# Two transformer blocks on one core: the list of a pair of experts turned in another PSUM bank, a fourth buffer for rounded expert weights, and first feed-forward products ahead of the second turning of the modulation rows

## The reference

```python
def swiglu(h, w13, w2):
    a, b = jnp.split(h @ w13, 2, axis=-1)
    return (jax.nn.silu(a) * b) @ w2

def half_ffn(x, g, shift, scale, gate, w13, w2):
    return x + 0.5 * gate * swiglu(modulate(x, g, shift, scale), w13, w2)

def grouped_moe(h, router_w, router_b, w_gate, w_up, w_down):
    ...                      # sigmoid router; two experts per token out of one group of four
    for e in range(N_EXPERTS):
        he = jax.nn.silu(t @ w_gate[e]) * (t @ w_up[e])
        y = y + combine[:, e:e + 1] * (he @ w_down[e]).astype(jnp.float32)
```

## Time and profile before

| | |
|---|---|
| median of 3 runs | 2240.47 us (2235.95 to 2245.8) |
| profiled execution: own time | 2240.65 us |
| its span, first to last instruction | 2238.9 us |
| busy share PE, DVE, ACT | 96%, 69%, 48% |
| mean granted TensorE clock | 0.989 |

### The profile page before, as it was taken

The page is one execution under the profiler, slowest core; times in us unless marked ns, Lnnn a source line. Parts: engine busy times, 40 slices in busy tenths (PEclk is TensorE's granted clock), DMA queues, the critical chain, the costliest instruction groups (busy, mean ns, idle before and its releaser), DMA issues.

```text
span 2238.9 us, 31572 instructions
## 1 busy us (share of the span) xinstructions
PE 2141.5 (96%) x13334; PEld 1898.6 (85%) x13334; DVE 1555.5 (69%) x1626; ACT 1081.2 (48%) x1197; POOL 6.7 (0%) x16
## 2 busy tenths in 40 slices
PE   9999999998999999989999999899999999999998
PEld 7888888768999999989999889777777888777777
DVE  4896676336867777747776555787787545787877
ACT  4222231336434534445444645566666555666665
POOL 0000000000000000000000000000000000000000
PEclk9999999999999999999999999999999999999999
DMA  8676867523878688645887333688887333777886
GB/s 320 203 243 240 291 214 255 215 74 120 303 292 301 228 295 308 223 151 207 298 300 268 133 113 132 241 304 304 306 318 293 113 114 113 281 296 297 322 306 226
DMA packets 143105, 535.25 MB, mean 239 GB/s; under 512 B 11744, under 2 KB 47912, under 8 KB 115184
## 3 DMA queue, kind: packets, MB, share of 16 engines
q1 hardware_dynamic: 141280, 524.33, 64.6%
q0 software_dynamic: 944, 5.72, 0.6%
q10 hardware_dynamic: 736, 3.12, 0.4%
HBM read 532.06 MB, written 1.06 MB: 238 GB/s over the span
## 4 chain that ended last, share of the span: by engine, by line
PE 74%; DVE 13%; ACT 8%; DMA 3%; issue 2%; SPq 0%; DVEq 0%; ACTq 0%
PE PS L988 16%; PE PS L914 11%; PE PS L1565 9%; DVE moe_low L2916 7%; PE PS L1060 7%; PE PS L1010 7%; PE PS L949 5%; PE PS L1600 5%; PE PS L1115 4%; ACT W_HIGH L2163 2%; DMA moe_ring<-moe_w 2%; ACT h_parts L2163 2%; DVE ring_low L2416 1%; PE PS L807 1%; PE PS L883 1%
## 5 line engine op out<-in xcount | busy, mean ns | idle before, releaser
L988 PE MATMUL PS<-h_parts,FFN_HIGH 128*128 128x256 f32 x2112 | 383.1, 284 | 2.9 <-DVE h_parts L2397 2.9
L2916 DVE TENSOR_TENSOR moe_low<-moe_ring,W_HIGH 128x2048 fp32r<-128x2048 f32 x128 | 293.1, 2291 | 81.6 <-ACT W_HIGH L2163 81.3
L988 PEld LDWEIGHTS PS<-h_parts,FFN_HIGH 128*128 128x128 f32 x2112 | 329.0, 192 | 3.7 <-issue 3.4
L988 PE MATMUL PS<-h_parts,ring_low 128*128 128x256 f32 x1056 | 298.7, 283 | 0.0
L2163 ACT ACTIVATE W_HIGH<-moe_ring 128x2048 fp32r<-128x2048 f32 x128 | 244.7, 1914 | 66.8 <-PE PS L1565 33.7
L2424 DVE TENSOR_TENSOR ring_low<-ring,FFN_HIGH 128x2048 fp32r<-128x2048 f32 x99 | 226.8, 2290 | 37.7 <-ACT FFN_HIGH L1827 37.6
L2455 DVE SCALAR_TENSOR_TENSOR roots<-CB,cond_rows,roots 128x1024 f32<-128x1024 f32 x186 | 238.4, 1282 | 9.0
L1827 ACT ACTIVATE FFN_HIGH<-ring 128x2048 fp32r<-128x2048 f32 x99 | 189.1, 1910 | 97.2 <-DMA ring<-down_w 87.6
L988 PEld LDWEIGHTS PS<-h_parts,ring_low 128*128 128x128 f32 x1056 | 202.6, 192 | 0.0
L1565 PE MATMUL PS<-moe_low,HXH 128*128 128x512 f32 x504 | 200.1, 397 | 0.0
L2916 DVE TENSOR_TENSOR moe_low<-moe_ring,h_parts 128x2048 fp32r<-128x2048 f32 x64 | 146.4, 2288 | 34.6 <-ACT h_parts L2163 34.4
(11 more groups left out here) (388 smaller groups left out, 4670.9 us busy)
## 6 DMA issues: line engine op xcount, KB each, us to landing
moe_ring<-moe_w SPq DMA_DIRECT2D x192, 1024.0 KB, 5.2
CB<-mod_rows SPq DMA_DIRECT2D x192, 512.0 KB, 5.8
ring<-up_w SPq DMA_DIRECT2D x88, 1024.0 KB, 4.9
ring<-lin_w SPq DMA_DIRECT2D x55, 1024.0 KB, 4.8
ring<-down_w SPq DMA_DIRECT2D x43, 1024.0 KB, 5.8
CB<-mod_dual SPq DMA_DIRECT2D x96, 128.0 KB, 2.6
ring<-mod_w SPq DMA_DIRECT2D x8, 1024.0 KB, 8.4
CB<-mod_rows SPq DMA_DIRECT2D x32, 128.0 KB, 2.7
```

The source lines that it names most:

```text
L988: return mm(PS[:, i % 2, h * S:(h + 1) * S], a[:, k, h * P:(h + 1) * P], b[:, k, :], start=start, stop=(k == KT - 1 and j == 2), skip_grou ...
L2916: tt(by_tile(moe_low[:, moe_slot(l, p), :]), by_tile(moe_ring[:, moe_slot(l, p), :]), w_high_tiles(p), ALU.subtract).then_inc(w_low, 1)
```

## The change

There are three edits.

1. `turn_list` of the next pair writes PSUM bank 2 instead of 3. TensorE waits ahead of it for `mo_g` of the odd expert's first half (bank 2 emptied by `gated(e, 0)`), and the wait for `mo_placed` moves from `gate_up(e, 2)` of the odd expert to `gate_up(e, 0)` of the next even one, the next writer of bank 2.
2. A third flat buffer of rounded parts, so four with `H_HIGH`. All `split` calls of ScalarE and VectorE stand where they stood, but handle the unit one further ahead (`+ 4` for `+ 3`), with one more split ahead of the loop over the experts. ScalarE's wait for the buffer is for the end of unit `p - 4`. The ring of loads keeps its five slots.
3. The two groups of spare products ahead of `up0` go. `up0` starts on the first half of the modulations, and `turn_rows(1)` stands behind the first six products (`k == 0`).

```diff
-        W_FLAT = [rounded(f"W_HIGH{i}", G_at + (at + i * UW) * 4, [P, UW]) for i in range(2)]
-        at += 2 * UW
+        W_FLAT = [rounded(f"W_HIGH{i}", G_at + (at + i * UW) * 4, [P, UW]) for i in range(3)]
+        at += 3 * UW
...
-            return (W_FLAT[i % 3][:, :].rearrange("p (k c) -> p k c", k=KT) if i % 3 < 2 else H_HIGH)
+            return (W_FLAT[i % 4][:, :].rearrange("p (k c) -> p k c", k=KT) if i % 4 < 3 else H_HIGH)
...
-                keep_busy(0, 4)
-                pe.wait_ge(mods_ready, 1)
-                turn_rows(1)
-                keep_busy(0, 8)
...
-                pe.wait_ge(mods_ready, 2)
+                pe.wait_ge(mods_ready, 1)
...
+                            if k == 0:
+                                turn_rows(1)
+                        last.then_inc(unit_done, 1)
+                        pe.wait_ge(mods_ready, 2)
...
-                    if i == 2 and e % 2 and q + 1 < PAIRS:
-                        pe.wait_ge(mo_placed, q0 + q + 2)
+                    if i == 0 and e and e % 2 == 0:
+                        pe.wait_ge(mo_placed, q0 + q + 1)
...
-                        turn_list(q + 1, 3)
+                        pe.wait_ge(mo_g, 2 * (e0 + e) + 1)
+                        turn_list(q + 1, 2)
...
-                    act.wait_ge(unit_done, u0 + p - 2 if p >= 3 else u0)
+                    act.wait_ge(unit_done, u0 + p - 3 if p >= 4 else u0)
...
-                    split(MOE_AT[e, 0] + 3)
+                    split(MOE_AT[e, 0] + 4)
                     gate(e, 0)
-                    split(MOE_AT[e, 1] + 3)
+                    split(MOE_AT[e, 1] + 4)
                     if e:
-                        split(MOE_AT[e - 1, 4] + 3)
+                        split(MOE_AT[e - 1, 4] + 4)
                         if e % 2 and q + 1 < PAIRS:
-                            listed(q + 1, 3)
+                            listed(q + 1, 2)
                         if e % 2 == 0:
                             outputs(q - 1)
-                        split(MOE_AT[e - 1, 5] + 3)
-                    split(MOE_AT[e, 2] + 3)
+                        split(MOE_AT[e - 1, 5] + 4)
+                    split(MOE_AT[e, 2] + 4)
                     gate(e, 1)
-                    split(MOE_AT[e, 3] + 3)
+                    split(MOE_AT[e, 3] + 4)
```

More of the change, by code:

```diff
@@ L926, in up0 @@
                                     last = part(h, k, j)
-                    last.then_inc(unit_done, 1)
+                        last.then_inc(unit_done, 1)
                     sums(0, i)
@@ L2206, in moe @@
                 listed(0, 5)
+                split(3)
                 for e in range(NE):
@@ L2976, in moe @@
                     gated(e, 0)
-                    split(MOE_AT[e, 1] + 3)
+                    split(MOE_AT[e, 1] + 4)
                     if e:
-                        split(MOE_AT[e - 1, 4] + 3)
+                        split(MOE_AT[e - 1, 4] + 4)
                         if e % 2 and q + 1 < PAIRS:
-                            placed(q + 1, 3)
+                            placed(q + 1, 2)
                         if e % 2 == 0:
                             outputs(q - 1)
-                        split(MOE_AT[e - 1, 5] + 3)
+                        split(MOE_AT[e - 1, 5] + 4)
                     if e % 4 == 0 and group + 1 < GROUPS:
                         lists(group + 1)
-                    split(MOE_AT[e, 2] + 3)
+                    split(MOE_AT[e, 2] + 4)
                     gated(e, 1)
-                    split(MOE_AT[e, 3] + 3)
+                    split(MOE_AT[e, 3] + 4)
                     if e % 2 == 0 and group + 1 < GROUPS:
```

## The result

| | before | changed |
|---|---|---|
| median of the runs, us | 2238.39 (4 runs, 2235.95 to 2245.8) | 2313.51 (4 runs, 2311.29 to 2320.72) |
| profiled execution: own time / span | 2240.65 / 2238.9 | 2320.72 / 2318.8 |
| mean granted TensorE clock | 0.989 | 0.971 |

The changed kernel is slower: ratio 1.0335, 95% interval 1.03 to 1.0371, 75 us by the medians. The forecast was 2274 us with 2300 as the high end of its range. The direction was forecast, the size was not.

The account below looks back on a forecast made before the run. TensorE, busy 96% of 2238.9 us, was taken to bound the kernel; 2240.65 - 2.5 (start) + 4 (odd halves) + 26 (even halves) + 6 (clock) = 2274 us. Its own range was 2252 to 2305, the stated range 2238 to 2300.

Parts of the forecast that it names:

- Edit 1, 23.2 us if nothing else is late: Mixtures, list in the other bank: 14 TensorE waits of 1.66 us for `placed` go, saving 23.2 us.
- Edit 3, -2.5: Program start: `up0` begins earlier, saving 2.5 us; bounds 0, if a later feed-forward chain takes it, and 2.7.
- Edit 2, the mechanism: Mixtures: splits wait for loads, some 30 us or more per mixture, delaying `gated` some 2.2 us and list compare 2.6.
- The clock, "+6, four of the 16": TensorE in the mixtures: four of 16 new waits bring half clock, 1.5 us each: +6 us, bounds 0 and 24.
- slower, by the clock: Rival: nearly every new wait brings 3.4 us at half clock, 2268 + 24 = 2292 us; inside the forecast's 0.70.
- The landing, 5.2 us: Expert loads in the mixtures: median time from issue to landing, 5.2 us, at least 4.7; used in both halves' terms.
- The odd halves, "14 x (L - 4.9)": Odd halves of the mixtures, L the landing: 14 x 0.3 = +4 us instead of -23.
- The even halves, 16 x 1.6 = 26: Even halves of the mixtures: late splits delay list compare and gathered rows, mean 1.6 us over 16 halves, +26 us.
- The range: Whole kernel: 2252 us (loads at 4.7, no clock lost) to 2305 (loads at 5.7, half of the clock cost).
- the case without change: Rival: VectorE catches up after late splits, only half of the 26 arrives; 2244 us, 2235 to 2250, chance 0.15.
- The faster rival, "the loads are in time": Mixtures: loads land before ScalarE reaches the split, edit 2 costs nothing, edits 1 and 3 win; 2215 us, chance 0.15.
- break-even of 4.3 us: Load landing in the mixtures at which 14 x -0.6 + 16 x 0.7 - 2.5 is about nothing, deciding the faster case.

Follow-up runs that it names:

- the spare products: Changed kernel plus eight unused products ahead of odd experts' turned products and ahead of the gathering that waits for the list: 2312.03 us, ratio 1.0306.

## Why the prediction was right in direction and wrong in size

- **Edit 1, 23.2 us if nothing else is late: right.** 23.0 alone by the medians, 19.7 by the lengths.
- **Edit 3, -2.5: right at its place, wrong in the end.** The first unit ends 2.5 us earlier; the median does not move (2244.89 against 2244.34). The bound of 0 "if a later chain takes it" is what the profile shows, at 1229 us rather than in the first feed-forward.
- **Edit 2, the mechanism: right.** The splits wait for loads: 72 and 77 us per mixture for "some 30 or more", in about 8 pieces per pair for "12 or so". The loss comes through `gated` ahead of the turned products of odd experts (2.98 for 2.2 in the half worked out), and through the list compare (2.68 for 2.6). Splits three ahead with the same buffers remove nearly all of it.
- **The clock, "+6, four of the 16": the step that failed.** 22 stretches of half clock in the mixtures for 2 before, 82 us more, worth some 35 us by the table above. I had only one wait in the trace of before to go by, 2.01 with a fall, and the 1.66 without one. The new waits are 1.8 to 4.6 us; of those of 2.2 and more, 20 of 24 have a stretch in or behind them. The rival "slower, by the clock" counted 24 us for it and ended at 2292, still short, since it priced one stretch per odd half and four list waits, and the even halves' other waits not at all.
- **The landing, 5.2 us: too short for the loads that matter, the second mis-sized term.** The 28 loads on the chain took 5.65 on average, which adds 13 us. The median of 5.2 is over all loads, also those that nothing waits for.
- **The odd halves, "14 x (L - 4.9)": the form right.** Before, odd halves took 18.4 to 18.5 us (and one 20.0); after, up to 20.1 in the first mixture and 22.1 in the second (sums of seven, the last of each mixture left out: 136.0 and 142.9 against 129.2 and 130.8). Of these 18.9 us of growth over 14 halves the form at L = 5.2 makes 3, where the forecast said 4; the longer landings (5.56 on average here) make 5 and the half clock 11.
- **The even halves, 16 x 1.6 = 26: right at its own landing.** The seven even halves went from 156.7 and 155.5 us to 179.9 and 187.1 in sum: 55 us over 14, 2.1 to 7.4 each. Without half clock and with landings of 5.2 the growth would be 23 (the rest of these halves taken from the kernel with loads of half the bytes), where 14 x 1.6 is 22; the longer landings (5.75) make 8 and the half clock 24.
- **The sum.** 3 and 23 for the landing as forecast, 13 for longer landings, 35 for the clock: the 74 us by which the mixtures grew. The clock's part is not won back by mending it alone, since the landings then grow, as the spare products show. Both go when the landing is no longer waited for: 98 us between distances three and four.
- **The range.** Its high end, 2305, does not follow from its terms: loads at 5.7 and half of the clock's 24 give 2240.65 - 2.5 + 45 + 12 = 2295. In the case without change, the -3 and the +9 are added with no row behind them; half of the 26 would be 13.
- **The faster rival, "the loads are in time", with its break-even of 4.3 us:** with landings of 3.7 the kernel is faster than before by 12 us (0.9931), not by the 25 of the rival. Of the 86 us by which that run's lengths are shorter than the changed kernel's, 50 are its 28 shorter landings (28 us per us of landing, where the forecast had 30) and 36 are the half clock. The Trainium skill's estimate from "DMA: Bandwidth & Descriptors" (on the anatomy of one DMA, a fit for the other way of issuing), 4.4 us per load, was below every landing of 1 MB from the experts' ring in these traces (4.7 at least), and its sum, 2244, was off by 69 us. The Trainium skill's rule in "Perfetto Trace Analysis" (on finding performance opportunities), that a repeated gap can mean too few buffers, was right of the bank: that edit alone ended the repeated 1.66 and gave 23 us. It was not right of the fourth buffer: splits four ahead alone cost 113 us, and the buffer with splits three ahead gave nothing clear of noise (2215.7 for 2220.8 us).

## What to carry to other kernels

Moving the consumer of a load further ahead only helps as far as the ring lets the load be issued earlier; count, for each buffer in the chain, which event frees it, and compare the time from the latest of them to the consumer with the transfer time. In engines that work in order, a step that waits for a load delays the small urgent steps queued behind it, and those are what the bound engine waits for: moving one of them ahead of the late split gave back 53 of the 75 us, but check what is then behind it, since the same move cost 25 us where the split was in time. When a sum forecasts a new repeated wait of more than 2 us on TensorE, let its upper bound hold a half-clock stretch for every one, and take the landing from the loads that stand on the chain rather than from the median of the stage. To take two causes apart in a finished trace, subtract the landings on the chain from the length of the stage and see what the rest goes with.

## What the runs showed of the hardware that was not expected

- Waits of 1.66 us, seven per mixture, left TensorE's clock at 2.4 GHz. Of the 24 waits of 2.2 to 4.6 us in the changed kernel's mixtures, 20 had 3.4 or 6.8 us at 1.2 GHz in or behind them, and each us of that cost 0.42 us. The length of a wait does not decide it: in the kernel with splits three ahead and the gate ahead, six of eight waits of 2.8 us had none, nor had the waits of 2.46 and 2.83 with splits three ahead alone. What decides is open.
- A load of 1 MB in the experts' ring takes 4.7 us at least; 5.2 to 5.6 at the median with five slots, 6.3 with six. In the changed kernel those on the chain took 5.65 on average. A load of 512 KB took 3.7, so half of the bytes saved 1.5 us of 5.2.
- A load issued earlier can take longer: at 1217 us one that was issued 3.75 us earlier took 6.79 us for 4.76. With it a lead of 3 us won at the start of the program was lost 1.2 ms later, at one wait for VectorE and the half-clock stretch behind it.
